# A transformer block on one Trainium2 core: modulation sums in other memory, order and five buffers; norm products of tiles 2, 3 and head pairs of tiles 0, 1 spaced wider

## The chip, the core and the metric

The kernel runs on one core of a Trainium2 chip. The metric is the device time in microseconds (us) of one execution. The kernel before took 2266.83 us in the median of three runs (2257.48, 2266.83, 2268.22).

## What is computed

A sequence of 512 tokens of width 1024 goes through two blocks, all in float32.

The **first block** is a gated delta-rule mixer with a pooling branch, followed by PEER, a lookup among 16384 experts:

```python
h = _rmsnorm(x, norm_mix_w[l])
proj = h @ w_in[l]
qkv = jax.nn.silu(_causal_conv(qkv, conv_w[l]))
q = _l2norm(q); k = _l2norm(k)
o = _chunk_gated_delta_rule(q, k, v, g, beta)
o = _rmsnorm(o, dn_norm_w[l]) * jax.nn.silu(z)
x = x + jnp.concatenate([o, pool_out], axis=-1) @ w_out[l]
x = x + _peer(_rmsnorm(x, norm_ffn_w[l]), w_query[l], sub_keys[l], expert_down[l], expert_up[l])
```

In `_peer` each token picks 16 experts for each of 8 heads: a query product, two sets of 128 key scores, the top 16 of each, the top 16 of their sums, then `act = gelu(x . expert_down[idx])` and a sum of `gate * act * expert_up[idx]`. So 512 x 128 rows of 2048 floats are gathered.

The **second block** has a modulation `mod = silu(c) @ ada_w + ada_b` (six rows of 1024: shift, scale and gate of the mixer and of the FFN), a stick-breaking attention with 16 heads of 64, and a SwiGLU FFN of width 2816. Each is put between a modulated norm and a gated norm. It depends on the first block in everything but the modulation.

## The kernel before

**Tiles and halves.** The tokens are four tiles of 128 (t = 0 to 3). The first block's mixer and queries, the **front**, run for half h = 0 (tiles 0, 1) and h = 1 (tiles 2, 3). `front_plan(h)` (L68) is a list of stages written by hand; every engine walks through the same list and does its own part of each stage. The third number of `add` says by how many positions a stage of h = 1 comes after the one before it.

**The gather loop.** The experts are fetched by 512 indirect transfers (`LOADS`, L2039 on GpSimd, POOL), one for each of 16 experts of 8 heads of 4 tiles; each brings 128 rows of 8 KB into one of 8 slots (`RING`, L60). For each gather n VectorE makes the product with the token rows (L2403), ScalarE the gelu and a 128x32 diagonal (L1711, L1715), and TensorE adds it to a sum in banks 6 and 7 of PSUM (`sums`, after every second n). Only then does the counter `slot_done` free the slot, for which gather n + 8 waits. n is called the position.

**What runs beside it.** The front of h = 0 has to be nearly done before the first gather. From query unit 7 of h = 0 on, all stages carry positions (`paced`, L246), counted in gathers; an engine does a stage when it has passed that position of its own loop. The stages of the front of h = 1 fill positions 19 to 225; the second block for tiles 0 and 1 fills positions 264 to 504 by `half_plan` (L277): the value products (`v`, from `VALUES_AT`), eight pairs of heads (`PAIRS_AT`, `PAIR_PACE`), the output product (`OUT_AT`), the mixing (`MIX_AT`) and the FFN (`FFN_AT`). Of a pair i, with its start at position at: TensorE q and k at at and at + 1, scores at + 4, rests at + 8, values at at + 14; ScalarE the copies of q and k (L1751, L1752) at + 3, abs, exp and ln (L1760 to L1764) at + 5, the exponential of the rests (L1770) at + 12; VectorE the softplus (L2362) at + 7. The second block for tiles 2 and 3 follows the loop.

**The modulation sums.** `silu(c) @ ada_w` is made on VectorE: 48 units of 128x1024 (512 KB each, stage `ad`), each multiplied by one column of c and added to one of three accumulators of 2048 columns (`ada_acc`, L439; L2324 for the first of a row, L2327 for the others; numbers 0 to 15 go to the first, 16 to 31 to the second, 32 to 47 to the third). Units go through 4 buffers, loaded by SyncE (SP, L752) which waits for `mfree` of the number that used the buffer. The second accumulator lies at 80 KB of the arena, the third at 88 KB. Chunk 1 of the delta rule lives at 80 to 100 KB, so VectorE waits before number 16 for the chunk's output (`o`). Stage `ar` then adds the 128 partitions up with a product with ones, stage `aw` turns the rows into columns (`modc`), which the loop reads at position 130.

**The end of the front of h = 0** (stages in order): chunk scan `s1`, `s2`, `s3` for chunks 0 and 1 with pool and z units (`pz`) between, `pm` (pool products), `wo` 0 to 3 (w_out with the pooled half), `os` (VectorE: reciprocal L2279 and two diagonals L2282), `ob` (TensorE: the diagonals times ones), `om` (VectorE L2288, L2289: scale the state's output), `wo` 4 to 7, `xa` (add to x), `ar`, `n1` (norm: ScalarE's squares L1548), `tr1` (transposes), `aw`, `q` and `sc` (queries and scores), `xr0` (replicate token rows), `sel` (top k of heads 0 and 1), and then the first gather. In front of a `wo` of this part three sums stand for each stage of 0 to 3.

**The norm products of the front** are stages `rd` and `mu`: VectorE makes a diagonal (L2207), TensorE multiplies it with ones, VectorE scales q and k of a chunk (L2212). In h = 1 they stand at positions 61 to 64. Behind them come for each of chunks 2 and 3 `ui`, `gr`, `mk` (decay masks on POOL L1988, TensorE, VectorE L2197, ScalarE L1607, POOL L1993), then the triangular inverse in levels.

**Order within an engine.** Each engine does its list in order and waits on counters of the others. SP issues all plain loads in the order of the same list. All TensorE instructions go through one helper, L888.

Two places where the position matters and which the diff doesn't show:

```python
# spread_rows(t, k): replicated rows of tile 1, at position 114
if t == 1:
    pe.wait_ge(s["state"], 3)
    pe.wait_ge(s["os"], 3)
# tile_norm(t, 0) on VectorE, for tile 0 at position 235
ve.wait_ge(s["prow"], 48)
```

The row that `prow` 48 counts is loaded by SP (L801) when the last query unit of h = 1 is used (position 224).

## Time and profile before

| | |
|---|---|
| median of 3 runs | 2266.83 us (2257.48 to 2268.22) |
| the profiled execution | 2263.32 us, its span 2261.5 us |
| instructions in the span | 26069 |
| front of h = 0, to the first gather's issue | 0 to 260 us |
| gather loop | 260 to 1813 us |
| second block of tiles 2, 3 | 1813 to 2261.5 us |

In the profile "busy" is the time in which an engine has an instruction at work, the bracket behind a row of a timeline is the time that the engine stood idle before it and who ended that. PE is TensorE (PEld its weight load), DVE VectorE, ACT ScalarE, POOL GpSimd.
### The profile page before, as it was taken

The page shows a single profiled execution, that of the slowest core. Times are in us where ns is not written, and L with a number is a line of the kernel's source. Part 1 is how long each engine was busy: PE and PEld are TensorE (multiplying, and loading weights), DVE is VectorE, ACT ScalarE, POOL GpSimd, SP SyncE. Part 2 cuts the span into 40 slices and gives each one's busy share as a digit, 9 for nine tenths or more (in the row PEclk, how much of TensorE's full clock was granted, in tenths as well). Part 3 has the DMA queues.
Part 4 walks back from the last instruction along what each step waited for, and adds up shares of the span by engine and source line. Part 5 has one row for each costly group of instructions (what it writes and reads, how often), then busy time and mean ns, then how long its engine had stood idle before and what let it go on. Part 6 is the DMA issues. An engine that isn't in the chain of part 4 may idle for free.

```text
span 2261.5 us, 26069 instructions
## 1 busy us (share of the span) xinstructions
PE 1762.8 (78%) x9120; PEld 1128.1 (50%) x9120; DVE 1328.9 (59%) x2912; ACT 893.8 (40%) x2387; POOL 857.5 (38%) x679
## 2 busy tenths in 40 slices
PE   7897887756577769645886784889888779887998
PEld 6783665423334426301354421445454356667997
DVE  4758558977798765666564566665555500533542
ACT  3111344443444433446355535533223321644443
POOL 1300243357675434354433344434344300024654
PEclk9998897867788889866988886999899889998999
DMA  7258599989999999999999899999999954013543
GB/s 266 85 179 282 198 417 399 417 320 370 371 396 418 418 418 417 418 416 394 404 409 344 335 420 419 419 418 418 419 418 419 399 180 132 17 69 118 186 186 112
DMA packets 114578, 726.10 MB, mean 321 GB/s; under 512 B 12944, under 2 KB 12944, under 8 KB 43152
## 3 DMA queue, kind: packets, MB, share of 16 engines
q0 software_dynamic: 73728, 536.90, 58.4%
q1 hardware_dynamic: 40720, 187.54, 22.2%
q8 instruction: 72, 1.18, 0.2%
q14 instruction: 58, 0.48, 0.1%
HBM read 720.20 MB, written 2.10 MB: 319 GB/s over the span
## 4 chain that ended last, share of the span: by engine, by line
PE 44%; DMA 21%; DVE 13%; ACT 8%; issue 7%; POOL 6%; DVEq 0%; SPq 0%; POOLq 0%; ACTq 0%; PEldq 0%
PE ps L888 44%; DMA arena<-in_experts,arena_u 20%; DVE arena L2403 5%; POOL arena L2039 4%; DMA arena<-in_w_ada 1%; ACT arena L1715 1%; ACT sel L1711 1%; DVE arena L2096 1%; DVE arena L2244 1%; ACT L1765 0%; ACT L1711 0%; POOL r_high L2066 0%; DVE arena L2327 0%; DVE selu L2127 0%; ACT L1557 0%
## 5 line engine op out<-in xcount | busy, mean ns | idle before, releaser
L888 PE MATMUL ps<-arena 128*128 128x256 f32 (+4 forms) x6088 | 1305.5, 521 | 354.5 <-ACT arena L1715 302.4
L888 PEld LDWEIGHTS ps<-arena 128*128 128x128 f32 (+2 forms) x6088 | 761.6, 176 | 853.1 <-ACT arena L1715 398.0
L2039 POOL DMA_INDIRECT arena<-in_experts,arena_u x512 | 601.7, 1175 | 852.6 <-PE ps L888 760.8
L2403 DVE CUSTOM_DVE_ANT_0 arena<-arena 128x1024 f32<-128x1024 f32 x512 | 648.6, 1274 | 365.3 <-DMA arena<-in_experts,arena_u 360.2
L1711 ACT ACTIVATE sel<-sel 128x1 f32<-128x1 f32 x512 | 102.4, 200 | 686.1 <-DVE sel L2403 685.2
L2066 POOL TENSOR_TENSOR r_low<-middle,r_low 128x1024 fp32r<-128x1024 f32 x48 | 122.2, 2551 | 252.4 <-ACT r_low L1866 252.4
L1715 ACT ACTIVATE arena<-arena,sel 128x32 f32<-128x32 f32 x512 | 164.5, 321 | 16.6
L888 PE MATMUL ps<-r_low 128*128 128x256 f32 (+1 forms) x1104 | 142.6, 293 | 11.7 <-POOL r_low L2066 6.0
L888 PE MATMUL ps<-arena,consts 128*32 128x512 f32 (+5 forms) x672 | 92.6, 457 | 70.3 <-POOL arena L2020 37.4
L888 PEld LDWEIGHTS ps<-r_low 128*128 128x128 f32 x1104 | 139.1, 196 | 15.1 <-POOL r_low L2066 6.8
L1704 ACT ACTIVATE arena<-consts,arena 128x32 f32<-128x32 f32 x512 | 120.7, 307 | 0.0
L888 PEld LDWEIGHTS ps<-arena,consts 128*32 128x32 f32 (+2 forms) x672 | 37.1, 137 | 141.0 <-POOL arena L2020 53.7
L1866 ACT ACTIVATE r_low<-middle 128x1024 fp32r<-128x1024 f32 x68 | 71.3, 1056 | 79.4 <-PE ps L888 61.0
L2013 POOL TENSOR_TENSOR sel<-sel 128x512 f32<-128x512 f32 x32 | 42.5, 1329 | 133.6 <-DVE sel L2136 133.0
L2433 DVE SCALAR_TENSOR_TENSOR upper<-ps,upper 128x896 f32<-128x896 f32 x16 | 17.5, 1091 | 117.6 <-ACT upper L1895 117.5
L2468 DVE TENSOR_TENSOR r_low<-middle,r_low 128x1024 fp32r<-128x1024 f32 x20 | 42.5, 2126 | 27.2 <-ACT r_low L1866 27.2
L1711 ACT ACT_TABLE_LOAD x45 | 57.7, 1283 | 0.8
L888 PE MATMUL ps<-r_low,r_high 128*128 128x512 f32 x240 | 54.9, 390 | 1.7 <-DVE r_high L2484 1.7
L1977 POOL TENSOR_TENSOR arena<-arena 128x512 f32<-128x512 f32 x28 | 38.2, 1373 | 39.7 <-DVE arena L2226 27.9
L888 PE MATMUL ps<-r_high 128*128 128x256 f32 (+1 forms) x232 | 49.8, 334 | 2.2 <-DVE r_high L2437 2.2
L888 PEld LDWEIGHTS ps<-r_low,r_high 128*128 128x128 f32 x240 | 45.0, 188 | 11.2 <-DVE r_high L2484 1.9
L2482 DVE TENSOR_TENSOR middle<-middle,ps 128x256 f32<-128x256 f32 x22 | 9.3, 421 | 70.1 <-ACT middle L1952 70.1
(247 smaller groups left out, 1511.7 us busy)
## 6 DMA issues: line engine op xcount, KB each, us to landing
arena<-in_w_front SPq DMA_DIRECT2D x88, 512.0 KB, 3.6
middle<-in_w_late SPq DMA_DIRECT2D x18, 2048.0 KB, 7.9
arena<-in_w_ada SPq DMA_DIRECT2D x48, 512.0 KB
arena<-in_w_qkv SPq DMA_DIRECT2D x48, 512.0 KB, 4.3
arena<-in_w_late SPq DMA_DIRECT2D x22, 1024.0 KB, 13.6
arena<-in_w_late SPq DMA_DIRECT2D x30, 512.0 KB
arena<-in_experts,arena_u POOLq DMA_INDIRECT x512
x<-in_x SPq DMA_DIRECT2D x4, 512.0 KB, 8.9
```

Of the source, the lines that this page charges most:

```text
L888: return nc.tensor.matmul(out_, lhsT, rhs, start=start, stop=stop_, skip_group_check=skip)
L1704: nc.scalar.activation(gated[:, m % 2, 32 * j:32 * j + 32], fold, ACT.Copy, scale=gq[:, i % 4, 4 * q + j:4 * q + j + 1]).then_inc(s["gated ...
L1711: own.step(nc.scalar.activation(gel[:, n % 8:n % 8 + 1], dots[:, n % 8:n % 8 + 1], ACT.Gelu))
L1715: nc.scalar.activation(diag[:, m % 4, 32 * j:32 * j + 32], gated[:, m % 2, 32 * j:32 * j + 32], ACT.Copy, scale=gel[:, n % 8:n % 8 + 1]).t ...
L1866: nc.scalar.activation(u_hi[u], raw_unit(u), ACT.Copy).then_inc(s["u_hi"], 1)
L1977: tt(Bm[lv % 2][c], Am[c], m4, ALU.mult).then_inc(s["bl"], 1)
L2013: tt(onehot, onehot, fidx.rearrange("p s (o a) -> p s o a", o=1).broadcast_to([P, 2, 16, 16]), ALU.mult).then_inc(s["fpk"], 1)
L2039: nc.gpsimd.indirect_dma_start(ring[n % RING], None, a["experts"], bass.IndirectOffsetOnAxis(ap=idxq[:, i % 4, k:k + 1], axis=0),).then_in ...
L2066: nc.gpsimd.tensor_tensor(u_lo[u], raw_unit(u), u_hi[u], ALU.subtract).then_inc(s["u_lo"], 1)
L2096: ins = stt(acc[:, sh:SH], px[:, 0:SH - sh], w(CW - 1 - sh), acc[:, sh:SH], ALU.mult, ALU.add)
L2403: nc.vector.tensor_tensor_reduce(r[:, 0:D], r[:, 0:D], xrep[k % 4], 1.0, 0.0, ALU.mult, ALU.add, dots[:, n % 8:n % 8 + 1]).then_inc(s["dot ...
L2468: tt(u_lo[u], raw_unit(u), u_hi[u], ALU.subtract).then_inc(s["u_ld"], 1)
```

## The change

Constants and places in memory: `ADA_SLOTS` is 5, the fifth buffer at 168 KB, where otherwise the normed rows of tiles 1 and 3 stand; the second accumulator moves to 104 KB, the third to 80 KB; the wait of VectorE for `o` is before number 32 instead of 16. The semaphore turns of the buffers that are used again later are counted accordingly.

Order: in the front of h = 0 the sums come earlier, fewer before the norm of the output. `ar` is done in two stages, around `n1` and `tr1`, both in bank 0 of PSUM, and `aw` in two at the query units 10 and 13 of h = 0, which are positions 8 and 14 of the loop. The rows' replication doesn't wait for `aw` any more, and gather 7 not for `gfree`.

Positions: `rd` and `mu` of h = 1 stand at 61, 63, 64, 65, 67, 68, 70 and 72 (before 61, 61, 62, 62, 63, 63, 64, 64), and every later stage of h = 1 comes 8 later: the copy of chunk 2's output at 115 (107), chunk 3's masks from 116 (108), its levels from 128 (120), w_out at 180 to 194 (172 to 186), query units at 201 to 232 (193 to 224), the last gate row at 257 (249). In the half plan: values at 269 to 277 (270 to 280), pairs from 280 every 8 (from 282 every 7), output product 354 to 368 (347 to 361), mixing from 369 (364), FFN unchanged from 387.

The diff, cut to its core:

```diff
@@ -56,7 +56,7 @@
 N_GATE = 4
-ADA_RUNS, ADA_SLOTS = 48, 4
+ADA_RUNS, ADA_SLOTS = 48, 5
@@ -123,13 +123,13 @@
     add("rd", 0, 1)
-    add("rd", 1)
+    add("rd", 1, 2)
     add("mu", 0, 1)
-    add("rd", 2)
-    add("mu", 1, 1)
-    add("rd", 3)
-    add("mu", 2, 1)
-    add("mu", 3)
+    add("rd", 2, 1)
+    add("mu", 1, 2)
+    add("rd", 3, 1)
+    add("mu", 2, 2)
+    add("mu", 3, 2)
     if h == 0:
@@ -170,25 +170,30 @@
                 add("pl", g)
+                run(1)
             add("pz", 4)
...
             add("s2", c, 2)
+            run(1)
             add("s3", c, 2)
+            run(1)
             if h == 0 and c == 0:
...
                 add("oc", c)
+            run(2)
...
             add("pm", g)
-            run(2)
+            run(1)
         add("zg", 1)
+        run(1)
     else:
@@ -207,23 +212,20 @@
             add("wo", k)
-            run(3)
+            run(2)
     add("os", 0, 1)
-    run(1)
     add("ob", 0, 1)
-    run(1)
     add("om", 0, 1)
-    run(1)
     for k in range(4 if h == 0 else 0, OUT_UNITS):
         add("wo", k, 2)
-        run(3 if k == 4 else 2)
+        run((3, 2, 2, 0)[k % 4])
     add("xa", 0, 2)
     if h == 0:
-        add("ar")
+        add("ar", 0)
     add("n1", 0, 1)
...
     if h == 0:
-        add("aw")
+        add("ar", 1)
     add("q", 0, 1)
@@ -240,6 +242,8 @@
             add("perm", 1)
+        if h == 0 and j in (10, 13):
+            add("aw", (j - 10) // 3)
     add("sc", Q_UNITS - 1, 1)
@@ -263,10 +267,10 @@
 AHP = AH // 2
-VALUES_AT, PAIRS_AT, PAIR_PACE = 270, 282, 7
+VALUES_AT, PAIRS_AT, PAIR_PACE = 269, 280, 8
 PAIR_END = PAIRS_AT + PAIR_PACE * (AHP - 1)
-OUT_AT = PAIR_END + 16
-MIX_AT = OUT_AT + 17
+OUT_AT = PAIR_END + 18
+MIX_AT = OUT_AT + 15
 FFN_AT, FFN_PACE = 387, 5
@@ -283,17 +287,17 @@
     for j in range(KD):
-        pe.append((VALUES_AT + 3 * j // 2, "v", j))
+        pe.append((VALUES_AT + 5 * j // 4, "v", j))
         if j % 4 == 3:
-            act.append((VALUES_AT + 3 * j // 2 + 2, "v", j // 4))
+            act.append((VALUES_AT + 5 * j // 4 + 2, "v", j // 4))
     for i in range(AHP):
         at = PAIRS_AT + PAIR_PACE * i
-        pe += [(at, "q", i), (at + 1, "k", i), (at + 4, "sc", i), (at + 8, "rs", i)]
+        pe += [(at, "q", i), (at + 1, "k", i), (at + 4, "sc", i), (at + 10, "rs", i)]
         act += [(at + 3, "qk", i), (at + 5, "ab", i)]
-        dve.append((at + 7, "sp", i))
+        dve.append((at + 8, "sp", i))
         act.append((at + PAIR_PACE + 5, "ex", i))
-        pe.append((at + PAIR_PACE + 7, "av", i))
-        act.append((at + PAIR_PACE + 8, "oc", i))
+        pe.append((at + PAIR_PACE + 8, "av", i))
+        act.append((at + PAIR_PACE + 10, "oc", i))
     for u in range(KD):
@@ -435,8 +439,8 @@
         narrow = [region(48 + 4 * n, D) for n in range(NARROW)]
-        ada_unit = [region(144 + 4 * n, D) for n in range(ADA_SLOTS)]
-        ada_acc = [gtrow[:, :, :].rearrange("p k n -> p (k n)"), region(80, 2 * D), region(88, 2 * D)]
+        ada_unit = [region(kb, D) for kb in (144, 148, 152, 156, 168)]
+        ada_acc = [gtrow[:, :, :].rearrange("p k n -> p (k n)"), region(104, 2 * D), region(80, 2 * D)]
         mod_rows = region3(60, 2, HALF)
@@ -565,15 +569,19 @@
+        def ada_turns(n):
+
+            return len(range(n, ADA_RUNS, ADA_SLOTS))
+
...
             n = h_slot(m)
-            before = sum(unit_slot(k)[0] == WIDE + n for k in range(QUERY0, 2 * FRONT)) if n < NARROW else ADA_RUNS // ADA_SLOTS
+            before = sum(unit_slot(k)[0] == WIDE + n for k in range(QUERY0, 2 * FRONT)) if n < NARROW else ada_turns(n - NARROW)
             return before + sum(h_slot(k) == n for k in range(m + 1))
...
-            before = ADA_RUNS // ADA_SLOTS if j % F_SLOTS < 2 else 0
+            before = ada_turns(2 + j % F_SLOTS)
             return before + j // F_SLOTS + 1
@@ -728,7 +736,7 @@
         h_unit = w_unit[WIDE:] + a_unit[0:2]
-        f_unit = a_unit[2:4] + [sem("f_unit")]
+        f_unit = a_unit[2:5]
@@ -1120,24 +1128,25 @@
                 elif stage == "xr0":
-                    pe.wait_ge(s["mod"], 4)
                     for k in range(8):
...
                 elif stage == "ar":
-                    pe.wait_ge(s["mfree"], ADA_RUNS)
-                    pe.wait_ge(s["os"], 2)
-                    for r in range(2):
-                        for q in range(4):
-                            ins = mm(ps[32 * q:32 * q + 32, 7 * r, :], const(C_ONES)[:, 0:32], ada_acc[1 + r][:, q * HALF:(q + 1) * HALF])
-                        ins.then_inc(s["gfree"], 1)
+                    r = arg
+                    if r == 0:
+                        pe.wait_ge(s["mfree"], ADA_RUNS)
+                        pe.wait_ge(s["os"], 2)
+                    else:
+                        pe.wait_ge(s["mod"], 1)
+                    for q in range(4):
+                        ins = mm(ps[32 * q:32 * q + 32, 0, :], const(C_ONES)[:, 0:32], ada_acc[1 + r][:, q * HALF:(q + 1) * HALF])
+                    ins.then_inc(s["gfree"], 1)
                 elif stage == "aw":
-                    for r in range(2):
-                        pe.wait_ge(s["mod"], r + 1)
-                        for j in range(4):
-                            ins = mm(ps[:, 7 * r, j * P:(j + 1) * P], mod_rows[:, r, j * P:(j + 1) * P], ident)
-                        ins.then_inc(s["gfree"], 1)
+                    pe.wait_ge(s["mod"], 2 + arg)
+                    for j in range(4):
+                        ins = mm(ps[:, 0, j * P:(j + 1) * P], mod_rows[:, arg, j * P:(j + 1) * P], ident)
+                    ins.then_inc(s["gfree"], 1)
                 elif stage == "gp":
@@ -1673,14 +1682,12 @@
                 elif stage == "ar":
-                    for r in range(2):
-                        sc.wait_ge(s["gfree"], r + 1)
-                        nc.scalar.activation(mod_rows[:, r, :], ps[:, 7 * r, :], ACT.Copy, scale=0.5).then_inc(s["mod"], 1)
+                    sc.wait_ge(s["gfree"], arg + 1)
+                    nc.scalar.activation(mod_rows[:, arg, :], ps[:, 0, :], ACT.Copy, scale=0.5).then_inc(s["mod"], 1)
                 elif stage == "aw":
-                    for r in range(2):
-                        sc.wait_ge(s["gfree"], 2 + r + 1)
-                        nc.scalar.activation(flat(modc)[:, 16 * r:16 * r + 16].rearrange("p (g j) -> p g j", g=4),
-                                             ps[:, 7 * r, :].rearrange("p (j g x) -> p g j x", j=4, g=4)[:, :, :, 0], ACT.Copy).then_inc(s["mod"], 1)
+                    sc.wait_ge(s["gfree"], 2 + arg + 1)
+                    nc.scalar.activation(flat(modc)[:, 16 * arg:16 * arg + 16].rearrange("p (g j) -> p g j", g=4),
+                                         ps[:, 0, :].rearrange("p (j g x) -> p g j x", j=4, g=4)[:, :, :, 0], ACT.Copy).then_inc(s["mod"], 1)
                 elif stage == "xr0":
@@ -2034,7 +2041,7 @@
                     pl.wait_ge(s["slot_done"], n - RING + 1)
-                elif n >= RING - 2:
+                elif n == RING - 2:
                     pl.wait_ge(s["gfree"], 2)
@@ -2317,7 +2324,7 @@
                         ve.wait_ge(s["cs"], 1)
-                    if k == 16:
+                    if k == 32:
                         ve.wait_ge(s["o"], 2)
...
                     if kd == 0:
```

## Rows read from the trace of the kernel before

**Rows 1.** The page: span, GB/s in its 40 slices, the gathers' queue (packets, MB, share).

```profile
span 2261.5 us, 26069 instructions
...
GB/s 266 85 179 282 198 417 399 417 320 370 371 396 418 418 418 417 418 416 394 404 409 344 335 420 419 419 418 418 419 418 419 399 180 132 17 69 118 186 186 112
...
q0 software_dynamic: 73728, 536.90, 58.4%
```

**Rows 2.** Stretches of the loop, products only: length, busy (xcount), PEclk, DMA share, GB/s.

```profile
462.00:512.00 50.00, 19.77 (x30) 0.60 0.81 305
512.00:600.00 88.00, 42.69 (x65) 0.77 0.97 382
600.00:662.00 62.00, 29.60 (x43) 0.81 0.95 365
662.00:938.00 276.00, 121.61 (x189) 0.90 1.01 418
...
1058.00:1094.00 36.00, 15.77 (x24) 0.81 0.95 361
1094.00:1196.00 102.00, 41.09 (x65) 0.89 1.00 404
1196.00:1304.00 108.00, 38.83 (x64) 0.83 0.88 345
```

**Rows 3.** Timeline of TensorE in the front: start, us, what, xcount, idle before.

```profile
176.66 16.21 PE L888 MATMUL ps<-arena 128*128 128x512 f32 x32 [0.77 <-ACT arena L1648]
202.12 3.43 PE L888 MATMUL ps<-arena,consts 128*128 128x512 f32 x4 [9.25 <-DVE arena L2282]
207.97 15.67 PE L888 MATMUL ps<-arena 128*128 128x512 f32 x32 [2.43 <-DVE arena L2289]
223.57 1.92 PE L888 MATMUL ps<-arena,consts 128*32 128x512 f32 x16
...
233.58 3.01 PE L888 MATMUL ps<-consts,arena 128*128 128x128 f32 x16
```

**Rows 4.** Timeline of VectorE in the front.

```profile
159.25 0.69 DVE L2276 SCALAR_TENSOR_TENSOR arena<-arena 128x512 f32<-128x512 f32 x1 [4.59 <-ACT arena L1644]
168.75 1.12 DVE L2256 SCALAR_TENSOR_TENSOR arena<-arena,gates,ps 128x128 f32<-128x128 f32 x4 [8.81 <-PE ps L888]
170.53 1.42 DVE L2324 TENSOR_SCALAR arena<-arena,ccol 128x1024 f32<-128x1024 f32 x2 [0.66 <-PE ps L888]
...
201.14 0.20 DVE L2279 RECIPROCAL arena<-arena 128x8 f32<-128x8 f32 x1
...
204.97 0.74 DVE L2288 SCALAR_TENSOR_TENSOR arena<-arena,vecs,ps 128x512 f32<-128x512 f32 x1
...
233.82 1.42 DVE L2310 COPY arena<-ps 128x256 f32<-128x256 f32 x4 [2.57 <-PE ps L899]
```

**Rows 5.** The chain that ended last, in the front.

```profile
171.98 5.34 DMA arena<-in_w_ada
```

**Rows 6.** A stretch of the front: length, busy of PE, PEld, DVE, ACT, POOL, PEclk, DMA, GB/s.

```profile
193.00:202.10 9.10, 0.00 (x0) 0.00 (x0) 6.20 (x8) 0.00 (x0) 0.00 (x0) 0.79 0.96 346
```

**Rows 7.** Timeline of ScalarE in the front.

```profile
225.56 0.60 ACT L1678 ACTIVATE arena<-ps 128x512 f32<-128x512 f32 x1 [0.26 <-PE ps L888]
226.06 1.05 ACT L1548 ACTIVATE arena<-x 128x1024 f32<-128x1024 f32 x1
```

**Rows 8.** Timeline of POOL at the norm products of tiles 2, 3.

```profile
475.35 0.94 POOL L2039 DMA_INDIRECT arena<-in_experts,arena_u  x1 [8.43 <-PE ps L888]
```

**Rows 9.** The load of the final norm's row, L801.

```profile
L801 SPq DMA_DIRECT2D arena<-in_prow x1: 328/328/328, 938.5 to 938.5; - x1
...
DMA to landing us min/median/max: 9.1/9.1/9.1
```

**Rows 10.** The pairs: L1770 (durations in ns, first and last start), and ScalarE's timeline.

```profile
L1770 ACT ACTIVATE arena<-ps x8: 810/810/811, 1143.7 to 1305.0; 128x768 f32<-128x768 f32 x8
...
1233.89 0.38 ACT L1751 ACTIVATE arena<-ps 128x256 f32<-128x256 f32 x1 [7.41 <-PE ps L888]
```

## The prediction

> **What bounds the kernel now.** I read the page first, then the stretches, then the waits inside the bad ones. The profiled run took 2263.32 us, its span is 2261.5, so 1.8 us lie around it; it is 3.5 us below the median of the three runs (2266.83, spread 10.7). A measurement of this kernel can tell about 0.5%, 11 us, from no change.
>
> The GB/s line of the page [rows 1] shows three parts: a front (0 to 262 us) with the DMA half idle, a loop of 512 gathers (262 to 1813), mostly at 418 GB/s, and a tail that the change doesn't touch (its numbers in both plans end where they did: the last block of the half plan is still at position 497). A gather is 536.90/512 = 1.049 MB, 2.51 us at 418 GB/s; a weight unit of 0.524 MB is 1.25 us. The loop's bytes are fixed, so it can gain only where the rate is below 418. The stretches [rows 2] give that: a stretch costs its length times (1 - rate/418): 462 to 512: 13.5 us; 512 to 600: 7.6; 600 to 662: 7.9; 1058 to 1094: 4.9; 1094 to 1196: 3.4; 1196 to 1304: 18.9; 662 to 938 nothing. The x of this view counts products, so positions follow: 63 products stand before 462, 313 before 1196.
>
> In the front what ends last is read from VectorE and TensorE. TensorE finishes its 32 products of the pooled half of w_out at 192.87 (176.66 + 16.21) and starts the norm products of the state output only at 202.12 [rows 3]. It waits for VectorE's diagonals, which follow a reciprocal at 201.14; before that VectorE works through modulation sums from 170.53 [rows 4], because in the kernel before number 16 must wait until the chunk scan has left its memory. VectorE had stood idle 4.59 us before 159.25 and 8.81 us before 168.75 [rows 4]. The sums also wait for loads: 5.34 us from a freed buffer to the next landed one, in the chain that ended last [rows 5]; with four buffers that is 4 sums in about 6.6 us (5.34 + 1.28), and by the plan it is 20 sums that fill 170.5 to 201.1.
>
> **The front, part by part.** Sums 16 to 31 go to memory that is free from the start, so they may run before the scan's end. The plan puts 4 beside the pools, 8 beside the scan and 4 beside the pool products; before it was none, none and 8. By 170 us VectorE has done 25 instead of 16: nine sums of 1.28 us (the tensor-scalar ones take 0.7, two in 1.42 [rows 4]) move into the idle time; their cover is those 13.4 us of idle time, more than their 11.5. VectorE's pieces of the scan get up to three sums ahead of them, 3.8 us inside the 4.59; without that cover each sum would cost its 1.28.
> Fewer sums also stand before the diagonals: numbers 0 to 40 instead of 0 to 35 in all, but 16 instead of 20 after 170 us. Five buffers make 5 sums in 6.6 us, 1.32 each. The first five have landed, so: 170.0 + 5 x 1.28 = 176.4, eleven more x 1.32 = 190.9. With the reciprocal and the first diagonal (0.9) that is 191.8, one us before TensorE is done. The wait of 9.25 us goes; what is late next is TensorE's own chain. I take 9.2; the low end is 6 (loads no denser than now for half of the sums).
> From first norm product to the next w_out product: 202.12 to 207.97, 5.85 us. VectorE's scaling starts at 204.97 there, behind two sums, which are gone from that place. After the idle time the four products ran at 0.86 each (3.43 for 4), the 32 that follow at 0.49 (15.67/32) [rows 3]; the granted clock was 0.79 in the idle stretch before [rows 6]. Without the idle time: 0.5 to 1.0 for the first product, 2.85 for the scaling (204.97 to 207.8), 0.2: 4.1. Saved 1.7 (0.9 to 1.9). The 32 products then: between 0 and 1.8 saved, by the clock; I take 1.0.
> Only one of the two row sums stays before the norm: ScalarE's squares began at 226.06 behind two copies of 0.60 [rows 7]; one goes, less its gap: 0.9. The transposes of the modulation rows, 16 products in 3.01 from 233.58 [rows 3], leave the place in front of the queries; the other row sum (half of 1.92, rows 3) takes it, under VectorE's copies that end at 235.24 (233.82 + 1.42 [rows 4]), where the queries then begin, not at 236.4: 1.3. The two transposes inside the loop are 8 products each, some 1.5 us of TensorE at positions 8 and 14, where 418 is held: 0; their reader is at position 130. SP's loads of sums are issued earlier, ahead of waits for units that are needed 30 us later: 0. The gather that waited for the second row sum (position 7) is freed, position 6 still waits for it, long done: 0.
> Front: 9.2 + 1.7 + 1.0 + 0.9 + 1.3 = **14.1** (9 to 16).
>
> **The norm products of tiles 2, 3.** At position 61 to 64 four diagonals, four products and four scalings stood in 4 positions. POOL shows what that did: no slot came free for 8.43 us until 475.35 [rows 8]. They now take 12 positions. The chain after them (growth, masks), with another dip near 490, keeps its spacing. Of 13.5 us I take 7 saved (2 to 11).
> All later stages of tiles 2, 3 move by 8 positions. Three things get closer. (1) At position 114 TensorE's replicated rows of tile 1 wait for the output copy of chunk 2, which moves from position 107 to 115: TensorE now stands there about one gather, and chunk 3's inner steps meet the turn of the tile. No row shows it; the nearest is the 7.9 us lost from 600 to 662; it may fall or grow by some 4: I take 1 lost. (2) The final norm's row is loaded after the last query unit, moved from position 224 to 232. Before, it was issued at 938.5 and took 9.1 us [rows 9]; the reader stays at position 235, so VectorE will wait some 5 us. Up to six gathers are in flight there, 15 us of DMA: 0 (up to 3 lost). (3) The gate rows keep their distance to the load and end at 257, before their reader at 264: 0.
>
> **The head pairs.** The value units start one position earlier and follow at 1.25 instead of 1.5 positions: the same 8 units against 11 instead of 12 gathers where 4.9 us are lost already [rows 2]: 1 lost (up to 4).
> Pairs come every 8 positions instead of 7, the rests 10 instead of 8 after the pair's start. The DMA needs 7 x 2.51 + 2 x 1.25 = 20.1 us per pair, 22.6 with 8. The eight exponentials run from 1143.7 to 1305.0, 23.0 us a pair [rows 10]: longer than 20.1, so the ring runs dry, most from 1196 on. ScalarE waits 7.41 us for TensorE at a pair's q and k [rows 10], and alike at the others, and holds the gates meanwhile; that distance does not change. But one more gather at 1.2 to 1.3 us of the engines brings a pair to about 24.3 against 22.6: the deficit per pair falls from 2.9 to 1.7, or 8 x 1.2 = 9.6; the wider places of the softplus and the rests should take some wait besides. Ends: 2 (deficit hardly moves) and 20 (all but 2.3 of the 22.3 lost from 1094 to 1304). I take **12**, the row nearest being the deficit's.
> The output units come at 354 to 368, the mixing at 369, before the FFN at 387: five positions of slack fewer, none was used at 418 GB/s: 0.
>
> **Sum:** 14.1 + 7 - 1 - 1 + 12 = 31 us. From the profiled run's 2263.3: 2232; from the median: 2236.
>
> **The rivals.**
> Front only (0.13). The loop's losses only change place: ScalarE's wait of 7.41 us per pair is untouched, and 418 GB/s may dip elsewhere. 2266.8 - 14 + 2 = 2255. Against: the dips stand where the plan is densest.
> Loads hold the front (0.08). If SP, which takes the loads in order, stands at a unit's wait while buffers are free, the diagonals come 6 us late, the rest as forecast: 2242. For it: SP has pool units between the sums.
> **Slower: the turn of tile 1** (0.05). TensorE stands at position 114 for state and copy, and from there to 137 chunk 3's steps, the replicated rows and the evacuation wait for each other. It decides where more than 15 us (six gathers) pass without a freed slot. Price: 24 positions at 1.5 us over the DMA's pace, 36 us, and 12 more from the pairs if they gain nothing: 2266.8 - 14 - 7 + 36 = 2282 at worst. Against: before, the same steps met the turn at positions 120 to 128 and lost 7.9.
> **The clock** (0.04). Between 462 and 512, where TensorE often waits, it was granted 0.60, at the pairs 0.89 and 0.83 [rows 2]. If wider spacing let the clock fall to the lower level (1.2 GHz) there, the q and k products of a pair, inside ScalarE's 7.41 us of wait, would take about 6.5 us more: 24.3 + 6.5 = 30.8 against 22.6, 66 us lost in eight pairs where 22.3 are now: 2266.8 - 14 - 7 + 44 = 2290. Against: 662 to 938 runs at the gathers' pace throughout, with weight products among them, and has 0.90 [rows 2]. The Trainium skill, TensorE: Matmul & The Clock Gate, section "HAM oscillation — how this bites in real kernels", says that short bursts of products with waits between them start each burst throttled; by that rule alone spreading work out is a loss. The trace agrees only where TensorE waits on other engines, not where it waits on the gathers.
>
> **How the numbers follow.** Forecast 0.70, rivals 0.13, 0.08, 0.05, 0.04. The terms' ends give 31 - 10 to 31 + 14 in the forecast's case; with both milder rivals inside at the upper end: 2221 to 2256. Faster by over 0.5% (below 2255.5): 0.69 of the forecast, 0.07 of the first rival, 0.07 of the second: 0.83; within: 0.11; slower: 0.06 (a third of the last two rivals' prices would still lie within).
>
> **What would show it.** Right: TensorE's wait before the norm products is under 1 us; the first gather is issued near 246 instead of 260; the stretch of positions 62 to 92 runs above 350 GB/s; in the pairs the rate is above 390. Wrong: the first gather after 252; a new dip at positions 114 to 137; pairs still 25 us or more with the rate at 345; a granted clock in the pairs below 0.7.

## The result and the profile after

The changed kernel took **2227.7 us** in the median of four runs (2224.5 to 2229.73), against 2264.76 for the kernel before in four runs beside it: ratio **0.9839** (95% interval 0.9818 to 0.986), 37 us less. The forecast was 2236 (2221 to 2256). The profiled executions are 34.1 us apart.

| | before | after |
|---|---|---|
| median us | 2264.76 (2266.83 in the three runs shown first) | 2227.7 |
| profiled execution, span | 2263.32, 2261.5 | 2229.22, 2227.4 |
| first gather issued | 260.0 | 245.3 |
| product of the last gather | 1813.2 | 1776.8 |
| from there to the end | 448.3 | 450.6 |

The page of the changed kernel, its span and the GB/s in 40 slices, which answers to [rows 1]:

```profile
span 2227.4 us, 26065 instructions
...
GB/s 281 85 255 217 262 418 400 417 367 379 367 364 419 418 417 418 418 416 397 392 418 419 418 420 419 412 419 418 419 418 419 373 160 119 1 93 97 189 189 113
```

The hole of 344 and 335 that stood near 1200 us [rows 1] is gone: from the 21st slice to the 31st all but one are at 418 to 420, and that one is 412. The hole of 320 near 470 us, with 370, 371 and 396 behind it, has become four slices of 364 to 379. The stretches, VectorE's products of the gather loop only (length, busy and count, granted clock, DMA share, GB/s), as in [rows 2]; a product leaves two records, so x49 are 24 to 25 positions:

```profile
445.00:511.00 66.00, 31.77 (x49) 0.61 0.96 375
511.00:592.00 81.00, 39.68 (x61) 0.77 0.98 375
592.00:657.00 65.00, 30.69 (x43) 0.84 0.94 347
1028.00:1080.00 52.00, 20.82 (x33) 0.79 0.94 367
1080.00:1292.00 212.00, 92.48 (x148) 0.86 1.01 418
1292.00:1334.00 42.00, 19.71 (x31) 0.95 1.02 420
1334.00:1749.00 415.00, 163.71 (x263) 0.91 1.01 416
```

Row by row these are: the norm products (positions 61 to 85), chunk 2's steps (85 to 115), the turn (115 to 136, around position 128, where the gathers pass from tile 0 to tile 1), the value units (264 to 280), the pairs (280 to 354), and what follows. How to turn them into time: a stretch loses its length times (1 - rate/418.5). Done with the bytes of each group of positions rather than with rounded rates, this gives a ledger in us lost. Here are the groups that matter; the loop's start (4.6 before, 4.9 after) and a group in the middle (1.0, 0.6) make up the rest of the sum. The first three groups move with their stages: in a kernel without the shift of 8 they are positions 61 to 77, 77 to 107 and 107 to 128.

| us lost | norm products | chunk 2 | turn | values | pairs | after the pairs | loop's end | all of the loop |
|---|---|---|---|---|---|---|---|---|
| before | 13.4 | 8.0 | 8.0 | 4.9 | 22.5 | 1.9 | 2.6 | 66.9 |
| after | 6.9 | 8.4 | 11.0 | 6.5 | 0.1 | 2.5 | 3.2 | 44.2 |

One execution stands behind each row. How far such figures scatter is seen in the seven kernels whose plan between positions 61 and 136 is the changed kernel's (it and e4 to e9 below; e8 moves two rows there): 5.7 to 8.1 at the norm products, 7.8 to 9.6 at chunk 2, 9.4 to 12.5 at the turn, 25.0 to 27.6 in all three. The three kernels with the old plan there (before, e1, e2) lost 29.2 to 29.9 in all.

So the profile's 34.1 us are 14.7 of an earlier first gather, 21.7 of a shorter loop (22.7 by the rate, 1.0 given back in slightly more bytes), less 2.3 lost behind the last product.

**The front**, TensorE's timeline of the changed kernel (start, duration, what, count, idle before), against [rows 3]:

```profile
175.38 16.22 PE L896 MATMUL ps<-arena 128*128 128x512 f32 x32 [0.76 <-ACT arena L1657]
191.44 1.88 PE L896 MATMUL ps<-arena,consts 128*128 128x512 f32 x4
195.57 15.67 PE L896 MATMUL ps<-arena 128*128 128x512 f32 x32 [2.25 <-DVE arena L2296]
211.17 1.06 PE L896 MATMUL ps<-arena,consts 128*32 128x512 f32 x8
216.85 3.16 PE L907 MATMUL ps<-consts,arena 128*128 128x128 f32 x16 [4.61 <-DVE arena L2313]
219.94 1.50 PE L896 MATMUL ps<-arena,consts 128*32 128x512 f32 x8
221.61 8.33 PE L896 MATMUL ps<-arena 128*128 128x256 f32 x40 [0.17 <-DVE arena L2317]
```

The second row carries no wait in brackets: the 9.25 us in front of the norm products are gone. VectorE's timeline says why:

```profile
183.47 6.38 DVE L2334 SCALAR_TENSOR_TENSOR arena<-arena,ccol 128x1024 f32<-128x1024 f32 x5 [0.16 <-DMA arena<-in_w_ada]
189.78 0.20 DVE L2286 RECIPROCAL arena<-arena 128x8 f32<-128x8 f32 x1
190.00 1.29 DVE L2289 TENSOR_TENSOR arena<-consts,arena 128x512 f32<-128x512 f32 x2
```

The reciprocal starts at 189.78 instead of 201.14 [rows 4], so the diagonals are ready when TensorE is done with w_out at 191.44.

**The pairs**, the exponential of each pair (durations in ns, first and last start), against [rows 10]:

```profile
L1777 ACT ACTIVATE arena<-ps x8: 811/811/812, 1125.2 to 1282.9; 128x768 f32<-128x768 f32 x8
```

That is (1282.9 - 1125.2)/7 = 22.5 us a pair, the 22.6 that the gathers and the two weight units of a pair need: the pairs now go at the DMA's pace.

Of the prediction's other signs, the first gather near 246 us (245.3), the wait under 1 us and the rate above 350 GB/s in the norm products (375) came too. One of its signs of being wrong came in part: from position 115 to 136 the rate is 347 GB/s, where the nearest stretch before had 365.

### The profile page after: what moved, and what is told of

Same layout as the page of the kernel before. It is cut to its first block, busy times and chain, and to the rows that moved or that the text cites. A ratio compares the mean times of both kernels' runs of the same rounds, so it can differ in the third digit from the quotient of the medians.

```text
span 2227.4 us, 26065 instructions
## 1 busy us (share of the span) xinstructions
PE 1753.5 (79%) x9120; PEld 1123.0 (50%) x9120; DVE 1324.5 (59%) x2912; ACT 895.5 (40%) x2387; POOL 844.9 (38%) x679
## 3 DMA queue, kind: packets, MB, share of 16 engines
q1 hardware_dynamic: 40720, 187.54, 22.4%
## 4 chain that ended last, share of the span: by engine, by line
PE 44%; DMA 23%; DVE 14%; ACT 7%; issue 6%; POOL 5%; DVEq 0%; SPq 0%; POOLq 0%; ACTq 0%; PEldq 0%
PE ps L896 44%; DMA arena<-in_experts,arena_u 22%; DVE arena L2410 6%; POOL arena L2046 4%; ACT arena L1722 1%; ACT sel L1718 1%; DVE arena L2103 1%; DVE arena L2251 1%; ACT L1718 0%; ACT L1566 0%; DVE arena L2250 0%; DVE selu L2123 0%; POOL r_high L2073 0%; DMA middle<-in_w_late 0%; ACT upper L1897 0%
## 5 line engine op out<-in xcount | busy, mean ns | idle before, releaser
L2046 POOL DMA_INDIRECT arena<-in_experts,arena_u x512 | 588.1, 1149 | 843.4 <-PE ps L896 750.9
L896 PE MATMUL ps<-arena,consts 128*32 128x512 f32 (+5 forms) x672 | 97.5, 483 | 50.6 <-POOL arena L2027 26.2
L896 PEld LDWEIGHTS ps<-r_low,r_high 128*128 128x128 f32 x240 | 45.0, 188 | 11.2 <-DVE r_high L2491 1.9
L2489 DVE TENSOR_TENSOR middle<-middle,ps 128x256 f32<-128x256 f32 x22 | 9.3, 421 | 69.1 <-ACT middle L1959 69.1
## 6 DMA issues: line engine op xcount, KB each, us to landing
arena<-in_w_late SPq DMA_DIRECT2D x22, 1024.0 KB, 13.8
```

The costliest lines, as they stand in the source:

```text
L896: return nc.tensor.matmul(out_, lhsT, rhs, start=start, stop=stop_, skip_group_check=skip)
L2046: nc.gpsimd.indirect_dma_start(ring[n % RING], None, a["experts"], bass.IndirectOffsetOnAxis(ap=idxq[:, i % 4, k:k + 1], axis=0),).then_in ...
```

## The experiments

Each kernel was timed beside the kernel before (medians 2260.8 to 2262.6 in these sessions). **e1 to e3** take the change apart. The theory is the prediction's: three gains that add up (14.1, 7 - 1, 12 - 1). The rivals: some of them only change place.

e1, the changed kernel with the old plan of the norm products and of the second block:

```diff
-    add("rd", 1, 2)
+    add("rd", 1)
...
-VALUES_AT, PAIRS_AT, PAIR_PACE = 269, 280, 8
+VALUES_AT, PAIRS_AT, PAIR_PACE = 270, 282, 7
...
```

> The sums' new memory, order, five buffers and the split row stages alone; norm products of tiles 2, 3 and head pairs as before. My account (the front gives its full amount to the end, as the loop is bound by the DMA): first gather near 245.3 us as in the changed kernel, 13 to 15 us off the time, about 2250; the loop loses 13.4 us at the norm products and 22.5 at the pairs as before. Rival (the front's gain is partly given back in the loop, and the pairs gain more because the front moved them): under 9 us off, and the losses at the pairs change by more than 4 us.

e2, the kernel before with the new plan of values and pairs alone:

```diff
-VALUES_AT, PAIRS_AT, PAIR_PACE = 270, 282, 7
+VALUES_AT, PAIRS_AT, PAIR_PACE = 269, 280, 8
...
```

> The kernel before with the value units' and head pairs' new positions alone. My account: DMA time lost from the first pair to the output product falls from 22.5 to under 2 us, the time by 19 to 23 us, about 2244. Rival (the wider norm products or the front's change share in the pairs' gain): the loss stays above 6 us and the time falls by 10 to 14 us, as the recorded prediction had it.

e3, the kernel before with the new spacing of the norm products alone:

```diff
-    add("rd", 1)
+    add("rd", 1, 2)
...
-    add("mu", 3)
+    add("mu", 3, 2)
```

> The kernel before with the norm products of tiles 2, 3 spaced wider alone (later stages of tiles 2, 3 move by 8 positions). My account: 6 to 7 us won at the norm products, 3 lost at the turn from tile 0 to tile 1, so 3 to 4 us off in all, about 2261, first gather at 260 and pairs losing 22 us as before. Rival (the loss at the turn comes from the front's change, not from the shift): 6 to 7 us off.

| | us (runs) | ratio [95%] | gain in the medians | lost: norm / chunk 2 / turn / values / pairs |
|---|---|---|---|---|
| e1 front only | 2247.85 (10) | 0.995 [0.9931, 0.9968] | 13.0 | 13.8 / 8.2 / 8.0 / 5.5 / 24.8 |
| e2 pairs only | 2244.0 (4) | 0.9936 [0.9914, 0.9957] | 16.8 | 13.1 / 8.5 / 7.6 / 8.4 / 0.1 |
| e3 norm products only | 2255.72 (10) | 0.9982 [0.9965, 0.9998] | 5.1 | 8.5 / 9.3 / 10.4 / 4.2 / 22.7 |

The gains are 13.0 + 16.8 + 5.1 = 34.9, and the whole change brought 33 to 37: within the intervals, some 4 us either way for each part, they add up. e1 lost 69.1 us in the loop, 2 more than the kernel before, so all but some 2 us of the front's gain got through it. e2 met its 2244 us, but its gain of 16.8 lies between the 19 to 23 of the account and the 10 to 14 of the rival: the pairs lose nothing any more, as the account said, and the values lose 8.4 instead of 4.9. By the ledger the pairs' part is the largest, 22.4 less 1.6 at the values, against 13.5 for the front; the medians have them in the same order, with intervals that overlap. e3 shows the small print of the norm products: 13.4 falls to 8.5 there, but chunk 2 behind them rises from 8.0 to 9.3 and the turn from 8.0 to 10.4, so its own ledger has 1.2 won. The 5.1 of its median (0.5 to 8 by the interval) is more than the ledgers bear out: from position 61 to 136 the kernels with the change's plan there, e3 with them, lose 25.0 to 28.0, those with the old plan 29.2 to 29.9.

**e4 and e5: order or buffers?** e4 keeps the new memory and five buffers, but the sums stand in the old places of the plan. e5 keeps the new order with four buffers.

```diff
                 add("pl", g)
-                run(1)
...
-            run(2)
+            run(3)
...
```

> The changed kernel with the sums in the old order (none beside the pools and the scan, eight beside the pool products, three behind each of the first output units, one behind each of three norm stages), in the new memory and with five buffers. My account (the order is what takes the sums out of the way of the norm's diagonals; five buffers only make them denser): 20 sums stand between 169 and the diagonals, at 1.32 us each, so TensorE waits about 5 us before its norm products instead of 0 (9.25 before), and scaling starts behind a sum; first gather 5 to 8 us later than in the changed kernel. Rival (buffers alone do it): within 1.5 us of the changed kernel.

```diff
-ADA_RUNS, ADA_SLOTS = 48, 5
+ADA_RUNS, ADA_SLOTS = 48, 4
...
-        ada_unit = [region(kb, D) for kb in (144, 148, 152, 156, 168)]
+        ada_unit = [region(kb, D) for kb in (144, 148, 152, 156)]
...
```

> The changed kernel with four buffers for the sums instead of five. My account (a sum comes every 1.65 us with four buffers where they stand together): the eleven sums ahead of the diagonals that had no landed buffer come some 3 us later, TensorE waits 2 to 4 us before its norm products, first gather 2 to 5 us later. Rival (the order alone does it, the fifth buffer is for nothing): first gather within 1 us of the changed kernel's 245.3.

TensorE's timelines, first e4's:

```profile
193.94 3.78 PE L894 MATMUL ps<-arena,consts 128*128 128x512 f32 x4 [4.01 <-DVE arena L2287]
199.80 16.88 PE L894 MATMUL ps<-arena 128*128 128x512 f32 x32 [2.07 <-DVE arena L2294]
```

and e5's:

```profile
195.19 1.98 PE L896 MATMUL ps<-arena,consts 128*128 128x512 f32 x4 [1.87 <-DVE arena L2289]
199.42 13.97 PE L896 MATMUL ps<-arena 128*128 128x512 f32 x32 [2.25 <-DVE arena L2296]
```

With the old order TensorE waits 4.01 us again, the norm products are slow (3.78 for four), and the 32 behind them take 16.88 instead of 15.67. Measured from a common marker, VectorE's first reciprocal of the norm products of chunk 0, to the first gather, which leaves out the program's start: 184.7 us before, 171.2 after, 178.6 in e4, 172.4 in e5. Over all the runs here the old front took 182.1 to 185.2 (before, e2, e3) and the new one 170.3 to 171.4 (nine kernels). So of 13.5 us the order is worth 7.4, as foreseen, and 6.1 is what e4 keeps (the row sums and transposes moved back, the new memory with the freer waits, and the buffer). The fifth buffer by itself shows 1.2 with the new order, less than the 2 to 5 expected and little more than the scatter. e5's wait of 1.87 us costs less than it looks, because the products behind it ran at full clock (13.97 us, where 15.67 came at a granted 0.89). The single times, 2230.96 and 2231.21 against the change's 2227.7, are both some 3 us longer, within what single runs scatter. By the front alone e4's would have been 7.4 longer, but its marker stands at 72.3 against 74.1, 1.8 us earlier, its loop lost 43.0 against 44.2 and moved 1.0 us less in bytes, and what follows the last product took 449.1 against 450.6.

**e6 and e7: pace or gaps?** e6 has 8 positions a pair with the old distances inside it, e7 7 positions with the new ones.

```diff
-        pe += [(at, "q", i), (at + 1, "k", i), (at + 4, "sc", i), (at + 10, "rs", i)]
+        pe += [(at, "q", i), (at + 1, "k", i), (at + 4, "sc", i), (at + 8, "rs", i)]
...
```

> The changed kernel with pairs every 8 positions, but inside a pair the old gaps: softplus at 7 instead of 8 behind the pair's start, rests at 8 instead of 10, values at 15 instead of 16. Theory pace (a ring that once runs dry makes each pair longer, and 8 positions keep it from running dry): pairs lose under 3 us of DMA time, the time is within 3 us of the changed kernel's. Theory gaps (the wider gaps take the waits away that made a pair long): 8 to 12 us are lost at the pairs, the time is 8 to 12 us longer than the changed kernel's.

```diff
-VALUES_AT, PAIRS_AT, PAIR_PACE = 269, 280, 8
+VALUES_AT, PAIRS_AT, PAIR_PACE = 269, 280, 7
```

> The changed kernel with pairs every 7 positions, the new gaps inside a pair kept. Theory pace: the ring runs dry as before, 18 to 25 us are lost at the pairs, the time is about 20 us longer than the changed kernel's. Theory gaps: under 12 us are lost at the pairs.

e6 took 2227.92 (four runs, ratio 0.9846 [0.9825, 0.9867]), e7 2244.17 (0.9909 [0.9882, 0.9937]); the pairs lost 3.8 us in e6 and 21.1 in e7. The pace decides; at 7 positions the new distances alone gain next to nothing. (e7's four runs lie between 2235.42 and 2251.0, and its profile is of the slowest; its median is 16.5 us above the changed kernel's, not the 20 expected.) ScalarE's timeline shows how the two states look, its copy of a pair's q once a pair. Before, the wait for TensorE grows from pair to pair (the first four pairs):

```profile
1117.54 0.38 ACT L1751 ACTIVATE arena<-ps 128x256 f32<-128x256 f32 x1 [2.35 <-PE ps L888]
1140.88 0.38 ACT L1751 ACTIVATE arena<-ps 128x256 f32<-128x256 f32 x1 [4.48 <-PE ps L888]
1163.56 0.38 ACT L1751 ACTIVATE arena<-ps 128x256 f32<-128x256 f32 x1 [6.16 <-PE ps L888]
1185.99 0.38 ACT L1751 ACTIVATE arena<-ps 128x256 f32<-128x256 f32 x1 [8.37 <-PE ps L888]
```

after it stays small (the second to the fifth pair):

```profile
1118.57 0.38 ACT L1758 ACTIVATE arena<-ps 128x256 f32<-128x256 f32 x1 [1.00 <-PE ps L896]
1143.27 0.39 ACT L1758 ACTIVATE arena<-ps 128x256 f32<-128x256 f32 x1 [1.94 <-PE ps L896]
1164.67 0.38 ACT L1758 ACTIVATE arena<-ps 128x256 f32<-128x256 f32 x1 [2.07 <-PE ps L896]
1187.81 0.38 ACT L1758 ACTIVATE arena<-ps 128x256 f32<-128x256 f32 x1 [1.45 <-PE ps L896]
```

and in e6 it grows as before while the DMA hardly suffers (the third to the sixth pair):

```profile
1144.93 0.38 ACT L1758 ACTIVATE arena<-ps 128x256 f32<-128x256 f32 x1 [3.78 <-PE ps L896]
1168.92 0.38 ACT L1758 ACTIVATE arena<-ps 128x256 f32<-128x256 f32 x1 [5.89 <-PE ps L896]
1192.80 0.38 ACT L1758 ACTIVATE arena<-ps 128x256 f32<-128x256 f32 x1 [6.00 <-PE ps L896]
1216.75 0.39 ACT L1758 ACTIVATE arena<-ps 128x256 f32<-128x256 f32 x1 [7.79 <-PE ps L896]
```

e6's pairs come every 23.9 to 24.0 us (1144.93, 1168.92, 1192.80, 1216.75), 1.4 more than the DMA needs. The compute falls behind by that much a pair, but the gathers already under way pay it: nothing is lost before position 320, and 3.7 us in the three groups of eight positions from there. At 7 positions a pair the debt is 2.9 us and more, and both the kernel before and e7 lose from position 304 on, after three pairs. As an estimate from these figures, the slots could pay some 7 us (five pairs at 1.4) to 9 us (three at 2.9), not the 20 us of eight full slots. Once they have run out a pair gets longer still: by the starts of these copies the pairs before came every 22.4 to 23.3 us at first and every 25.3 to 26.1 at the end. The new distances inside a pair bring it from 23.9 to the 22.5 above, which is the DMA's pace; that is worth the 3.8 us of the ledger (under 3 was expected), and no difference in the medians (2227.92 and 2227.7).

**e8: is the turn's loss TensorE's stand at position 114?** In the prediction this was the place that got closer. e8 moves tile 1's replicated rows four positions later.

```diff
-                return TOPK * PH - (9 if bank_xr(t, k) == 5 else 14 - k)
+                return TOPK * PH - (9 if bank_xr(t, k) == 5 else (10 if t == 1 else 14) - k)
```

> The changed kernel with the first two replicated rows of tile 1 at positions 118 and 119 instead of 114 and 115, so that TensorE comes to them after the output copy of chunk 2. If TensorE's wait there is what costs 3 us more at the turn than before, the DMA time lost from position 115 to 136 falls from 11.0 to about 8. Rival (chunk 3's stages meeting the turn cost it): it stays above 10.

It took 2230.72 (one run), and the turn lost 10.4 us instead of 11.0, within the scatter of 9.4 to 12.5 and not the 8 expected. The stand at 114 is not what costs. The longest wait of TensorE's timeline at the turn is another, in the changed kernel:

```profile
634.40 1.11 PE L1006 MATMUL ps<-consts,arena 128*128 128x128 f32 x4 [7.78 <-POOL arena L1984]
```

POOL makes that mask product behind the gathers of its position. It was not held by a slot there: from 626.53 on it issued four gathers with at most 0.30 us between them, and started the product at 633.07. e11 below takes this wait away, and the turn loses as much as before.

**e9: half a step back.** 7.5 positions a pair, values at 1.5 positions each again.

```diff
-VALUES_AT, PAIRS_AT, PAIR_PACE = 269, 280, 8
+VALUES_AT, PAIRS_AT, PAIR_PACE = 269, 283, 7.5
...
-        pe.append((VALUES_AT + 5 * j // 4, "v", j))
+        pe.append((VALUES_AT + 3 * j // 2, "v", j))
...
```

> The changed kernel with the value units every 1.5 positions again (269 to 279), pairs from 283 every 7.5 positions, the new gaps inside a pair kept, everything from the output product on as it was. Theory pace (a pair of the new gaps takes the engines about as long as the DMA's 22.6 us at 8 positions, so 7.5 positions, 21.3 us of DMA, make a deficit of about 1 us a pair, most of which the ring's 8 slots pay): under 5 us lost at the pairs, 1 to 3 won at the value units, the time within 3 us of the changed kernel's. Rival (any pace under 8 lets the ring run dry for good): 10 us or more lost at the pairs, the time 8 to 12 us longer.

2228.68 (four runs, ratio 0.9851 [0.9825, 0.9876]): the values lost 5.2 instead of 6.5, the pairs 4.0 instead of 0.1, from position 312 on. The time is the same, as the account had it. Its pairs took 22.2 us on average (the first to the seventh exponential, 1131.5 to 1264.8), so with the new distances the engines can do a pair in less than the 22.6 us that the DMA takes for one of 8 positions.

**e10 to e12: the spacing, and POOL's place.** e10 spaces the norm products by one position each instead of two every second time, so that all behind them moves by 4 instead of 8. e11 lets POOL do its stages two positions earlier, ahead of an issue that waits for a slot. e12 does both.

```diff
-    add("rd", 1, 2)
+    add("rd", 1, 1)
     add("mu", 0, 1)
     add("rd", 2, 1)
-    add("mu", 1, 2)
+    add("mu", 1, 1)
...
```

> The changed kernel with the norm products of tiles 2, 3 over 8 positions (61 to 68) instead of 12, so that later stages of tiles 2, 3 move by 4 instead of 8. My account (the loss at the turn, 8.0 before and 11.0 after, comes from where chunk 3's stages stand against the turn's rows): it falls to 8 to 9, the loss at the norm products rises from 6.9 to 8 to 10, the time stays. Rival (3 us of difference at the turn are a matter of the execution): it stays at 10 to 12.

```diff
-                front.upto(n - RING + GROUP - 2)
+                front.upto(n - RING + 2 * GROUP - 2)
```

> The changed kernel with POOL doing its front stages two positions earlier in the loop. TensorE stood 7.78 us at the turn for a mask product of chunk 3 that POOL makes after the gathers of that position, and 3 to 5 us at each growth product of chunks 2 and 3. My account (POOL, held by the ring, comes too late to its stages): TensorE's waits for POOL shrink to under 3 us each, 4 to 10 us less are lost between positions 61 and 136, the time falls by as much below the changed kernel's. Rival (POOL only waits for others in its turn, and gathers are issued later behind that wait): no less is lost, or up to 5 us more.

> The changed kernel with both edits that came out faster: norm products of tiles 2, 3 over 8 positions and POOL's front stages two positions earlier. If they work on different waits (the one moves chunk 3 away from the turn's rows, the other takes TensorE's waits for POOL in chunk 2's steps), under 3 us are lost in chunk 2's steps and about 8 at the turn, and the time is 2208 to 2214 us. If both remove the same waits in chunk 2's steps, the time is that of the better one, 2216 to 2219.

| | us (runs) | ratio [95%] | first gather | lost: norm / chunk 2 / turn / values / pairs / loop |
|---|---|---|---|---|
| after | 2227.7 (4) | 0.9839 [0.9818, 0.986] | 245.3 | 6.9 / 8.4 / 11.0 / 6.5 / 0.1 / 44.2 |
| e10 | 2216.81 (1) | | 242.3 | 7.7 / 2.0 / 7.7 / 7.3 / 0.1 / 37.7 |
| e11 | 2219.09 (4) | 0.9812 [0.9784, 0.984] | 241.1 | 8.5 / 0.2 / 12.1 / 5.7 / 0.1 / 36.8 |
| e12 | 2222.04 (6) | 0.9827 [0.9805, 0.9849] | 245.1 | 9.8 / -0.1 / 8.9 / 9.0 / 0.2 / 40.0 |

The stretches of e11, norm products, chunk 2's steps and the turn, read as the seven of the changed kernel above:

```profile
441.00:505.00 64.00, 32.70 (x49) 0.61 0.94 364
504.00:577.00 73.00, 37.03 (x57) 0.78 1.01 417
577.00:643.00 66.00, 29.52 (x44) 0.79 0.89 345
```

Chunk 2's steps take 73 us at 417 GB/s instead of 81 at 375. Nothing but POOL's order was changed, and chunk 2 lost 0.2 where seven kernels with the old order lost 7.8 to 9.6: that POOL's place matters there is shown. Through which wait is not. In that stretch TensorE waited only 2.3 us for POOL in the changed kernel (1.0 in e11); what fell is POOL's own waiting for a free slot, from 23.4 to 14.8 us. Over all of positions 61 to 136 TensorE's waits for POOL fell from 22.6 to 15.0 us, the longest from 7.8 to 4.5 and not under the 3 expected. The norm products and the turn lost 2.7 more, so 5.6 us are back from position 61 to 136.

At the turn the wait of 7.78 us is gone in e11, the same product follows without a wait:

```profile
615.83 1.90 PE L896 MATMUL ps<-arena,consts 128*32 128x512 f32 x16
617.66 0.66 PE L1006 MATMUL ps<-consts,arena 128*128 128x128 f32 x4
```

and the turn lost 12.1 us, no less than before. So that wait is not what costs there, and what does is open.

e10 was expected to keep its time and was 11 us faster in its one run; its 2.0 at chunk 2 was not expected. Why four positions less of shift do there what POOL's order does is open. In e10 and e12 the groups end at positions 81, 111 and 132; up to 136, where the changed kernel's turn ends, they lost 1.5 and 2.2 us more. From 61 to 136 the four kernels of the table lost 26.4, 18.9, 20.8 and 20.8 us. And the two edits do not add: e12 met neither of the times that were expected of it: it was 3 us slower than e11 in the medians (2222.04, 2219.09), inside what the intervals allow, with more lost at the values (9.0) and the norm products (9.8).

**A version that came out ahead of both kernels** is e11: 2219.09 in four runs (2215.13 to 2221.92), all below the changed kernel's four (2224.5 to 2229.73), but in another session. By the ratios to the kernel before, 0.9812 and 0.9839, it is 6 us ahead of the changed kernel, and their intervals overlap (0.9818 to 0.984), so this lead is likely and not certain. The profiled executions are 11.4 us apart (2217.84 and 2229.22): 3.3 of these stand already at the marker in the front (70.8 and 74.1), which the edit has no part in, 0.8 come from there to the first gather, and the ledger has 7.4. e10's single 2216.81 has the same early marker (70.9) in it, and 6.5 in the ledger.

## Why the prediction was right, and where a term was off

**The front, 14.1 forecast, 13.5 measured** from the common marker (10.7 to 14.9 by the scatter given above), 13.0 in e1's median. Term by term from the two timelines:

| | forecast | measured |
|---|---|---|
| wait before the norm products | 9.2 | 9.4 (25.46 to 16.06 from the start of w_out) |
| norm products and scaling | 1.7 | 1.72 (5.85 to 4.13) |
| the 32 products of w_out behind | 1.0 | 0 (15.67 both) |
| a row sum's copy ahead of the squares | 0.9 | 0.86 |
| transposes out of the queries' way | 1.3 | 1.55 |

The missed one is the clock: the idle time went, and the four products ran at a granted 1.00, but the next 32 at 0.89 as before. The remaining 1.2 of the first gather's 14.7 us are there already at the common marker (75.3 and 74.1), ahead of all these terms.

**The norm products, 7 forecast, 6.5 measured**, and **the turn, 1 lost forecast, 3.0 measured**. The net, 6, stands against 3.1 in the ledger (6.5 - 3.0, and chunk 2 loses 0.4 more), 1.2 in e3's ledger and 5.1 in its median. The size was within the ends given (some 4 either way), the reason given for it, TensorE's stand at position 114, fell with e8. Up to the end of the turn the loss goes with the shift of the stages: 7.6 to 8.0 without one, 9.2 with 4 (11.2 in e12, with POOL earlier), 9.4 to 12.5 with 8. Which wait it is stays open.

**The final norm's row, 0 forecast.** VectorE stands where it was foreseen to wait for the row (the profile names no releaser), and the gathers go on:

```profile
948.52 1.28 DVE L2358 SCALAR_TENSOR_TENSOR x<-x,stat,arena 128x1024 f32<-128x1024 f32 x1 [3.72 <-issue]
```

3.72 us where 5 were forecast, at 419, 414 and 418 GB/s in the three stretches of 10 us from 930 on.

**The value units, 1 lost forecast, 1.6 measured.** With the new places the kernels here lost 5.7 to 9.1 us in them, with the old ones 4.2 to 5.6.

**The pairs, 12 forecast, 22.4 measured**, above the end of 20: this is the step that failed. It took the deficit of a pair (24.3 us of engines against the DMA's 22.6) as time lost, for each of eight pairs. Two things were wrong with it. A deficit is lost only when the slots have run out, and 1.4 us a pair takes five pairs for that; e6 lost 3.8 in all, not the 10.3 that the forecast left. And the wider distances inside a pair, entered as "some wait besides", bring the pair to 22.5, the DMA's pace. The 24.3 itself was close to e6's 23.9 to 24.0 by luck, for two errors cancel in it. The 23.0 us a pair were read from the starts of the exponentials, whose last interval is only 16.1 us because no pair follows; by the starts of the copies a pair took 24.0 (1117.5 to 1285.3). And the 1.2 added for one more gather do not show: with it e6's pairs are no longer than that. The forecast's sign that the rate in the pairs would be above 390 was right; it was 418.

**The sum** was 31 and came out at 34.1 in the profiles and 37 in the medians. Against the terms the profiles have 10.4 more at the pairs and 1.2 more before the marker; 0.6 less in the front, 2.9 less at norm products, chunk 2 and turn, 0.6 less at the values; and, in places where nothing was forecast, 0.3 + 1.2 lost at the loop's start and behind the pairs, 1.0 in bytes, 2.3 behind the last product (0.4 won in the middle). That is 31 + 11.6 - 8.5 = 34.1. That the total was nearer than its largest term is luck: the pairs brought almost twice what was forecast, and the small terms all erred to the other side.

**The rivals.** Front only: e2 and e3 show the other two parts by themselves, so it falls. Loads hold the front: VectorE's waits for loads in the sums before the reciprocal are now 0.16 to 0.89 us each; it falls. The slower turn: the turn did get slower, by 3 us and not 36, and not through the stand at 114. The clock: 0.86 granted in the pairs (0.89 and 0.83 before [rows 2], 0.86 over both) at the gathers' pace, so wider spacing took nothing from it. The rule of the Trainium skill (TensorE: Matmul & The Clock Gate, section "HAM oscillation — how this bites in real kernels") that a long enough wait makes the next burst of products start throttled agrees with the front, where e4's wait of 4.01 us is followed by four products in 3.78 us against 1.88 without a wait; in the pairs the wider spacing did not bring it on. The prediction took the throttling as absent where TensorE only keeps the gathers' pace; that reading was too wide. From 950 to 1058 us of the kernel before, where TensorE waited 43.3 us for ScalarE's diagonals in the gather loop, it was granted 0.64 while the DMA moved 416 GB/s: the clock fell there and cost next to nothing.

## What to carry to other kernels

In a loop whose pace a DMA stream sets, write the ledger first: length less bytes over the sustained rate, by group of positions. Work laid beside the stream costs nothing while a group's engine time is within its transfers, and a deficit is paid out of the filled slots before it costs anything; so the number to compare is the deficit times the count of groups against the slots' slack, not the deficit alone, and one position more a group can end the whole loss. Where the engine that issues the transfers also makes another engine's input, try that work ahead of the issues and look at the ledger: e11's one line took 8 us of loss out of chunk 2's steps. The longest wait in a bad stretch need not be its cause: the 7.78 us at the turn went and the loss stayed.

## What had not been expected of the hardware

The same instructions at the program's start took different times in different executions. The first 32 projection products, first the kernel before, then e1, then e3, whose plans are the same up to there:

```profile
15.06 9.95 PE L888 MATMUL ps<-arena 128*128 128x256 f32 x32 [1.92 <-DVE arena L2164]
```

```profile
15.09 7.14 PE L896 MATMUL ps<-arena 128*128 128x256 f32 x32 [1.92 <-DVE arena L2171]
```

```profile
15.00 8.63 PE L888 MATMUL ps<-arena 128*128 128x256 f32 x32 [1.92 <-DVE arena L2164]
```

What follows comes earlier or later with it: the marker in the front stands at 75.3 us before, 72.3 in e3, whose code is the same up to there, 70.9 in e1, 74.1 in the change. The 32 products are only part of it: they took 8.83 in the change and 8.69 in e11, whose markers are 3.3 us apart. In all it is up to 4.8 us (70.8 in e11, 75.5 in e5), about the spread of the changed kernel's four runs, and it is the reason to measure the front from a marker and not from zero. The granted clock is 1.00 from 15 to 25 us in these three (0.68 to 0.81 from 15 to 22 us in the change), so what makes the difference stays open. Further in, the clock does account for it: w_out's 32 products took 13.97 us at a granted 1.00 (e5), 15.67 at 0.89 and 16.88 at 0.83 (e4), each time 13.9 to 14.0 when multiplied.
